# Eighteen whole weight chunks beside the adaLN units instead of six in pieces, and six output blocks parted over the contraction

## What is computed

```python
mod = jax.nn.silu(c) @ ada_w[l] + ada_b[l]              # (9, 2048) @ (2048, 12288)
sh1, sc1, g1, sh2, sc2, g2 = jnp.split(mod[:, None, :], 6, axis=-1)
h = rms_norm(x) * (1.0 + sc1) + sh1
proj = h @ w_in                                          # (288, 2048) @ (2048, 18448)
hq, hf, hi, hg, mq, mk, mv, mi, mf, mo, ga, gb = jnp.split(proj, ...)
# lf = log_sigmoid(mf + bias), ig = mi + bias: the gates; then HGRN2 and mLSTM on these,
# x = x + g1 * (merged @ w_out), a ConvFFN with w_up and w_down, and a last rms_norm
```

## Time and profile before

| | us |
|---|---|
| median of three runs | 2286.97 (2285.03 to 2287.28) |
| span of the profiled execution | 2286.7 |
| PE busy, whole span | 2227.3 (97%) |
| DVE busy, ACT busy, POOL busy | 1091.9, 992.9, 319.4 |
| transpose of the gate rows, the mark at the end of the first stage | starts at 247.41 |

### The profile page before, as it was taken

The page is one execution under the profiler, slowest core; times in us unless marked ns, Lnnn a source line. Parts: engine busy times, 40 slices in busy tenths (PEclk is TensorE's granted clock), DMA queues, the critical chain, the costliest instruction groups (busy, mean ns, idle before and its releaser), DMA issues. The chain is left out here.

```text
span 2286.7 us, 42270 instructions
## 1 busy us (share of the span) xinstructions
PE 2227.3 (97%) x17436; PEld 2084.4 (91%) x17436; DVE 1091.9 (48%) x1454; ACT 992.9 (43%) x1365; POOL 319.4 (14%) x455
## 2 busy tenths in 40 slices
PE   6899999999999999999999997999999999999998
PEld 2489999999999999999999986999999999999997
DVE  1245455464464544444444555555555555544443
ACT  3245553563554334444434445443444343433333
POOL 1010212211221222120211223000000000110000
PEclk8899999999999999999999999999999999999999
DMA  9977676666656576766675779555555555555553
GB/s 344 366 242 220 182 211 186 205 187 206 211 183 198 178 231 194 237 213 205 202 233 180 227 240 317 179 159 172 160 168 160 168 162 166 176 164 172 169 169 107
DMA packets 407411, 460.03 MB, mean 201 GB/s; under 512 B 14844, under 2 KB 379956, under 8 KB 406434
## 3 DMA queue, kind: packets, MB, share of 16 engines
q1 hardware_dynamic: 394192, 410.64, 57.9%
q0 software_dynamic: 12240, 46.03, 6.5%
q10 hardware_dynamic: 833, 1.26, 0.2%
HBM read 431.48 MB, written 26.39 MB: 200 GB/s over the span
## 5 line engine op out<-in xcount | busy, mean ns | idle before, releaser
L697 PE MATMUL ps<-xh,whi 128*128 128x288 f32 x3968 | 1193.4, 301 | 9.8 <-issue 6.2
L1575 DVE TENSOR_TENSOR wlo<-raw,whi 128x1024 fp32r<-128x1024 f32 x584 | 731.3, 1254 | 977.2 <-ACT whi L1161 968.2
L699 PE MATMUL ps<-xh,wlo 128*128 128x288 f32 x3968 | 1172.2, 295 | 0.0
L698 PE MATMUL ps<-xl,whi 128*128 128x288 f32 x3968 | 1171.2, 295 | 0.0
L1161 ACT ACTIVATE whi<-raw 128x1024 fp32r<-128x1024 f32 x584 | 616.5, 1057 | 803.2 <-PE ps L699 773.1
L697 PEld LDWEIGHTS ps<-xh,whi 128*128 128x128 f32 x3968 | 746.7, 188 | 63.2 <-issue 58.9
L698 PEld LDWEIGHTS ps<-xl,whi 128*128 128x128 f32 x3968 | 746.8, 188 | 0.0
L699 PEld LDWEIGHTS ps<-xh,wlo 128*128 128x128 f32 x3968 | 746.5, 188 | 0.0
L697 PE MATMUL ps<-ffh,whi 128*128 128x288 f32 x704 | 209.2, 297 | 0.0
L699 PE MATMUL ps<-ffh,wlo 128*128 128x288 f32 x704 | 208.4, 296 | 0.0
L698 PE MATMUL ps<-ffl,whi 128*128 128x288 f32 x704 | 208.3, 296 | 0.0
(11 more groups left out here) (393 smaller groups left out, 1583.6 us busy)
## 6 DMA issues: line engine op xcount, KB each, us to landing
raw<-in_w_in SPq DMA_DIRECT2D x288, 512.0 KB, 4.3
raw<-in_w_up SPq DMA_DIRECT2D x176, 512.0 KB, 3.6
raw<-in_w_down SPq DMA_DIRECT2D x88, 512.0 KB, 3.5
araw<-in_ada_w SPq DMA_DIRECT2D x74, 512.0 KB, 5.4
raw<-in_w_out SPq DMA_DIRECT2D x32, 512.0 KB, 3.5
uraw_x<-in_ada_w SPq DMA_DIRECT2D x30, 512.0 KB, 8.7
uraw<-in_ada_w SPq DMA_DIRECT2D x24, 512.0 KB, 10.2
top<-in_ada_w SPq DMA_DIRECT2D x24, 512.0 KB, 8.0
```

Source lines behind the costliest of these rows:

```text
L697: mm(o, whi[:, s, kk, cols], hi[:, kt0 + kk, :], start=first and kk == 0, stop=False)
L698: mm(o, whi[:, s, kk, cols], lo[:, kt0 + kk, :], start=False, stop=False)
L699: x = mm(o, wlo[:, s, kk, cols], hi[:, kt0 + kk, :], start=False, stop=last and kk == KC - 1)
L1575: TT(wlo[:, s], raw[:, s], whi[:, s].bitcast(F32), ALU.subtract).then_inc(lo_done, 1)
```

## The change

It works on the first stage alone.

- **Beside the units** stand 18 chunks (`EARLY`) instead of six: PE runs them whole, none or one behind a quarter, from unit 2 on (`BESIDE` = 2). 16 run behind quarters (2, 3, 3, 3, 3, 2 in units 2 to 7), two behind the last unit turn.
- **Six blocks part by part.** Chunks 0 to 23 (`PARTED`) are part 0 of blocks 0 to 5, then part 1 of all six, and so on, so that the first chunks need group 0 alone. Each chunk is its own PSUM group in bank k % 2. Part 0 is copied to `SQ` by ACT, parts 1 to 3 are added to it by DVE (`early_add`, two instructions), and each must be done before chunk k + 2 may write the bank. Chunks 24 to 39 are blocks 6 to 9 as before.
- **Loads.** SP loads chunks 0 to 3 before unit 2, 4 to 7 before unit 3, and 8 to 19 one at a time between the loads of units 4 to 7 (and the end of unit 3), each behind its wait for the low part of chunk k - 4.
- **x.** PE transposes three blocks behind each quarter of unit 0 and four ahead of it; DVE copies them; ACT squares the rows of x with a sum along the row, DVE puts the sums on a diagonal, PE sums with 3 matmuls of 128, 128 and 32 columns in place of 4 of 288. The turn of unit 1 follows that unit directly.
- **POOL** stores `xT` (2.25 MB) after unit 1 and not after unit 7's third quarter, since `SQ` lies over it; the loads of the gates' weights stay where they were.
- **Later** in the stage: gate matmuls from chunk 19, rows of the gates at chunks 23 to 26, `hg_front` at chunks 22 to 30.

```diff
-EARLY = 6
-HG_FIRST = "s" * EARLY + "sssssaa" * 6 + "ssss"
+EARLY = 18
+PARTED = 24
+HG_FIRST = "s" * EARLY + "sssaa" * 6 + "ssss"
...
-    return (n % 2, n // 2) if first and n < 8 else (n // length, n % length)
+    return (n % 6, n // 6) if first and n < PARTED else (n // length, n % length)
...
-BESIDE = 3
-X_AHEAD = 2
-EARLY_PIECES = (0, 1, 1, 2, 1, 1, 1, 1, 0, 1, 1, 2, 1, 1, 1, 1, 0, 2, 2, 2)
+BESIDE = 2
+X_AHEAD = 4
+EARLY_PIECES = (0, 4, 0, 4, 4, 4, 0, 4, 4, 0, 4, 4, 4, 0, 4, 4, 4, 0, 4, 4, 4, 0, 4, 0)
+EARLY_LOADS = 20
+def pieces_ahead(u, h):
+    return sum(EARLY_PIECES[:4 * (u - BESIDE) + h])
+def chunk_ends(u, h):
+    return range(pieces_ahead(u, h) // 4, pieces_ahead(u, h + 1) // 4)
+def loads_ahead(u, c):
+    return RING if u == BESIDE else min(EARLY_LOADS, 2 * RING + pieces_ahead(u - 1, c // 2) // 4)
...
-GATES = 10
+GATES = 19
+ROWS = 23
+FRONT = 5
...
# PE, early chunks
-                    yield from pieces(k + 1, k, part == 0, False, b, xh, xl, KC * part)
+                    pe.wait_ge(bank_free[k % 2], k // 2 + FREE)
+                    yield from pieces(k + 1, k, True, True, k % 2, xh, xl, KC * part)
...
# ACT, beside the units
+            def early_chunk(n):
+                if n < 6:
+                    act.wait_ge(used, n + 1 + FREE)
+                    to_padded(early_tile(n), n % 2)
+                if n + RING < EARLY + LEAD:
+                    hi(N_HG, n + RING)
+            for u in range(BESIDE, UNITS):
+                for h in range(4):
+                    if h == 0 and u in (4, 6):
+                        modulate(1, merged, 0, KT, (u // 2 - 1,))
+                    if h == 3:
+                        unit(u)
+                    for n in chunk_ends(u, h):
+                        early_chunk(n)
...
# DVE
+            def early_add(n):
+                dst, src = early_tile(n), early_bank(n)
+                dve.wait_ge(used, n + 1 + FREE)
+                TT(dst[:, :, 0:TP], dst[:, :, 0:TP], src[:, :, 0:TP], ALU.add)
+                TT(v, v, src[:, :, TP:T].rearrange(...), ALU.add).then_inc(bank_free[n % 2], 1)
...
+            unit(UNITS - 1)
+            k = pieces_ahead(UNITS, 0) // 4
+            early_add(k)
             samples(1, merged, 3, 0, KT)
             low_parts(1, merged, 3)
...
# POOL
-            pool.wait_ge(u_used, 4 * UNITS - 1)
+            pool.wait_ge(u_used, 4 * BESIDE)
             (store of xT, clearing of SQ's padding)
+            pool.wait_ge(u_used, 4 * UNITS - 1)
             (loads of gw, gb, m0)
```

More of the change, by code:

```diff
@@ L120 @@
 N_HG = (0, 0)
+FIRST_PAIRS = PARTED // 2 + 2
 def hg_base(i):
-    return ahead(N_HG, i, 40, 5)
+    return ahead((40, FIRST_PAIRS), i - 1, 40, 5) if i else N_HG
 N_ML = hg_base(4)
@@ L544, in build, with early_bank, early_tile @@
         bias_row = par[:, 0, :]
+        junk = merged[:].rearrange("p a b -> p (a b)")
+        diag = junk[:, 2 * D:2 * D + T]
+        def early_bank(n):
+            return ps[:, n % 2]
+        def early_tile(n):
+            b = place(n, 4, True)[0]
+            return SQ[:, b // 2, 2 * (b % 2):2 * (b % 2) + 2, :]
         rowpad = merged[0:MH, 1:3, :].rearrange("p a b -> p (a b)")[:, 0:TPAD]
@@ L560, in stage @@
                     if kind == "s":
-                        if first and n < EARLY:
+                        if first and n < EARLY_LOADS:
                             continue
@@ L607, in early_load @@
                 load(k, win_v, KC * part, hg_cols(0)[b])
-            for u in range(1, UNITS):
+            for c in range(UC):
+                unit_load(1, c)
+            loaded = 0
+            for u in range(BESIDE, UNITS):
                 for c in range(UC):
+                    for k in range(loaded, loads_ahead(u, c)):
+                        early_load(k)
+                    loaded = loads_ahead(u, c)
                     unit_load(u, c)
-                    if u % 2 == 0 and c % 4 == 3:
-                        early_load(u - 2 + c // 4)
+            for k in range(loaded, EARLY_LOADS):
+                early_load(k)
             hg_stage(0, first=True)
@@ L821, in unit @@
                     x.then_inc(u_used, 1)
-                    if h == 0 and u:
+                    if h == 0 and u not in (0, BESIDE):
                         unit_turn(u - 1)
                     tiles(h)
+                if u == BESIDE - 1:
+                    unit_turn(u)
             def unit_turn(u):
@@ L853, in tiles @@
                         x.then_inc(small_t, 1)
-                    if u == 2 and h == 0:
+                    if u == 1 and h == 0:
                         pe.wait_ge(sq_sum, 3)
-                        for kt in range(4):
-                            x = mm(ab[:, 0:T], ones[:, :], merged[:, kt, :], start=kt == 0, stop=kt == 3)
+                        for t in range(3):
+                            w = P if t < 2 else TS
+                            x = mm(ab[:, P * t:P * t + w], ones[0:w, :], diag[0:w, P * t:P * t + w], start=True, stop=True)
                         x.then_inc(ms_done, 1)
@@ L1043, in _ @@
             pe.wait_ge(ada_free, UNITS + FREE)
-            stream(hg_base(0), HG_FIRST, A_HG, late(GATES, gates(0, "", 0, 0)), xparts=0, start=True)
+            stream(hg_base(0), HG_FIRST, A_HG, late(GATES, gates(0, "", 0, 0)), start=True)
             pe.wait_ge(row_d, ROW_T)
@@ L1237, in conv_state @@
                 A(cst[:, :, 8 * g:8 * g + 8].rearrange("p f r -> p r f"), ab[:, 0:8 * FT].rearrange("p (r f) -> p r f", f=FT), ACT.Copy).then_inc(small_c, 1)
+            act.wait_ge(ld_x, 48)
+            for t in range(3):
+                w = P if t < 2 else TS
+                if t == 2:
+                    act.wait_ge(sq_done, 1)
+                A(junk[0:w, D * (t % 2):D * (t % 2 + 1)], xtm[0:w, t, :], ACT.Square, accum_out=ssx[0:w, t:t + 1]).then_inc(sq_done, 1)
             unit(0)
-            unit(1)
             act.wait_ge(const, 7)
@@ L1305, in stream @@
                     b, part = place(n, 4, start)
-                    if part == 3 and evict is not None:
+                    if start and n < PARTED:
+                        pass
+                    elif start and n == PARTED + 6:
+                        act.wait_ge(used, N[0] + n - 2 + FREE)
+                        evict(6, 0)
+                    elif part == 3 and evict is not None and not (start and b == 6):
                         act.wait_ge(used, N[0] + n + 1 + FREE)
@@ L1310, in stream, with hg_evict @@
                         each(n)
[L1312 to L1317 removed]
+            def hg_evict(g):
                 def evict(u, b):
[L1319 to L1322 removed]
+                    if u == 0:
                         act.wait_ge(hg["cp"], 2 * g)
[L1324 removed]
+                    if u == 4:
                         act.wait_ge(hg["vc"], g)
@@ L1439, in hook @@
                 hg_front(q, 0, True)
[L1440 removed]
+            stream(N_HG, HG_FIRST, A_HG, hg_evict(0), hook, start=True)
             act.wait_ge(row_t, 1)
@@ L1851, in hook, with each @@
                 gate_rows(q)
-                hg_front(q, 0)
-            stream(N_HG, HG_FIRST, A_HG, hook, start=True)
+                hg_front(q - FRONT, 0)
+            def each(n):
+                if n < PARTED:
+                    early_add(n)
+            stream(N_HG, HG_FIRST, A_HG, hook, each, start=True)
             dve.wait_ge(hg["zero"], 3)
```

178 lines of the change are left out of this document (84 added, 94 removed).

## The result

| | before | after |
|---|---|---|
| median of the runs (four each) | 2287.02 us | 2307.71 us (2304.15 to 2308.34) |
| ratio to the kernel before, 95% interval | | 1.0086, 1.0071 to 1.0100 |
| span of the profiled execution | 2286.7 us | 2306.0 us |
| mark: transposes of the gate rows | 247.41 us | 265.19 us |

What follows compares the result with a forecast made beforehand. PE was taken to bound the kernel, and narrowly the end of the units over DMA. A gain of 12.4 us there less 2.8 of waits behind gave 9.6 us: 2277 us from 2286.97, range 2270 to 2286.

Steps and rivals of the forecast that it cites:

- SP's queue: Beside the units, twelve single weight loads each hold a unit's loads 2.1 us, with 5 us of room: cost 0.
- after the units: Behind the units, PE may wait in three places, together 2.8 us, bounds 0 and 8.
- the 85.0: PE's time from the 18th chunk's end to the mark at 247.4, so the change breaks even at 162.4 us.
- term (c): At chunks 23 to 29, ACT's rows, tables and logarithms delay whi, so PE waits 0.9 us for wlo at chunk 29.
- End of the units at 150.0: The 18th chunk ends at 150.0 us, bounded by PE, against 162.4: 12.4 us gained, bounds 17.5 and 6.
- An early chunk is worth 3.2 us: Each chunk moved beside the units saves PE 3.2 us behind them, from 102 matmuls of 0.134 us each.
- evictions by DVE are hidden: 18 DVE sums of 0.9 us each, 16 us in all, hide under PE's 3.2 us a chunk: cost 0.
- rival 4: Beside the units, low parts over 5 us late make unit loads late; twelve waits of 2.1 us: 25 us, 2302, chance 0.07.
- Rival 3: PE waits for DMA at unit starts, falls to 1.2 GHz, loses 3.4 us in each of units 4 to 7: 2291, chance 0.07.
- (a): At the first gate matmul after chunk 19's first piece, PE waits 1.7 us for DVE's gwl.
- (b): Chunk 18's second half needs the second xl at 7.8 and is due at 7.9: 0.2 us.
- rival 2: ACT's pile at chunks 23 to 28 costs 8 us instead of 2.8: 2282, chance 0.14.

Runs made afterwards that it cites:

- e1: Changed kernel with SP's list alone reordered behind the units, ada_w pairs 2 to 6 four weight loads later: 2289.37 us, ratio 0.9997 to the kernel before.
- e13: Changed kernel with SP's list alone reordered, ada_w pairs three weight loads later instead of e1's four: 2289.26 us, ratio 0.9998 to the kernel before.
- e12: e9 plus 40 dummy matmuls ahead of unit 3, with SP's pairs three weight loads later, not four: 2278.98 us, ratio 0.9955 to the kernel before.
- e6: e1 plus 40 dummy matmuls ahead of unit 3's first quarter, results unused: 2287.12 us, ratio 0.9991 to the kernel before.
- e9: e1 with gate rows two chunks earlier and DVE's mod sum and gwl moved forward in its list: 2284.24 us, ratio 0.9979 to the kernel before.

## Why the prediction was wrong

**The step that failed** is the part "SP's queue", and with it the term "after the units". SP's list was looked at where the diff moves it, beside the units, and priced at 0 with a rival for it. Behind the units the only lines of the diff that change SP's list are `EARLY` = 18 and `"sssaa"` for `"sssssaa"`. The prediction took that as a shorter list of chunks, and counted the pairs on PE alone (1.07 us each, inside the 85.0). That each pair is also a load that waits for PE, with the next weights behind it, and that two chunks fewer between two pairs take 6.4 us from the room for that, was in no term and in no rival. The trace of the kernel before has the wait already (SP, 122 to 248 us):

```profile
SPq L577 <- PE ab L722: 31.7, 5, 7.4
```

That wait was free, and how near it was to not being so was not asked. Instead of 2.8 us, PE lost about 26 between the 18th chunk (154.0) and the mark (265.19), which are 111.2 us apart and not 85.0: 19.1 us of waits in the list and some 7 us of low clock behind them. e1 and e13 give 15 and 19 us of them back at the mark by SP's order alone (16.7 and 17.5, counted from the last unit turn). The rest is mostly term (c) below.

**The terms one by one.**

- *85.0 us of PE's work after 18 chunks, break-even at 162.4*: right. In e12 the last unit turn is at 144.90, two chunks and the turn later it is 152.4, and the mark comes at 239.19: 86.8 us, of which 1.0 are waits.
- *End of the units at 150.0*: 4.0 us early. The 18th chunk ends at 154.0 (last unit turn at 146.52, 0.9 for the turn and two chunks). Unit 3's first quarter came at 68.75 (forecast 67.2). From there to unit 4's first quarter 19.25 us passed, with the low clock that had been charged once; in e6, where the clock stayed at 1.00, it was 14.85, near the 14.7 of the forecast, so the low start cost 4.4 here (3.0 in e1), and 3.4 was forecast. The other units took 15.1 to 15.9 us. PE bounded them, as forecast, and from unit 4 on it waited for no load.
- *An early chunk is worth 3.2 us; evictions by DVE are hidden*: right; no wait for a bank over 0.3 us up to 180 us.
- *SP's single waits beside the units, rival 4*: cost 0. The sign that was named for it is there, SP's waits for `wlo` with a fall to 218 GB/s from 80 to 86 us, but PE waited for no load behind it. Rival 4's trigger was sought at the right engine and in the wrong stretch: the time it gave (2302) was near the truth for a reason that it did not have.
- *Rival 3, the clock low at every unit*: did not occur in the changed kernel beyond unit 3's start (e1 had it once more, at 94.91). The Trainium skill (TensorE: Matmul & The Clock Gate, HAM oscillation) describes that case for a kernel whose bursts are shorter than its DMA waits; with three chunks in a unit there were no such waits, and the stretches from 80 us on are at full clock. It did occur behind the units, where idle times of 4.6, 5.5 and 5.3 us lie in stretches with a mean clock of 0.91, 0.83 and 0.83.
- *(a) gwl 1.7 us*: 0.79. *(b) 0.2*: nothing. *(c) the pile of ACT, 0.9*: too small. With SP's order mended it costs 4.36 us of waiting for `mod` and some 3.4 us of low clock behind it (e13: 0.88 and 0.95 in 180 to 220 us), 7.8 us, which is the size of rival 2. The mark of e9, without that wait, is 7.0 us earlier than e13's; by the medians the two edits to the rows and to DVE's list give 4 us (e1 and e9). The error in it: only `whi` and `wlo` were followed through the pile. DVE's `mod` sum stands at its end too, and PE's next pair waits for it. The Trainium skill (PSUM — Partial Sum Buffer, Engine vs sequencer instructions) says that the queues of ScalarE, VectorE and GpSimd are strictly first in, first out; the rows of e13 agree, with an instruction of 0.15 us that ran 7.4 us after PE had its input ready.

**What was right** is the idea of the change, and in part its size. With SP's and DVE's lists mended and no dummy matmuls (e9) the kernel is 4.8 us faster than the kernel before, about half of the 9.6 us of the sum. With the dummy matmuls, which the kernel before did not get, and pairs three loads later (e12) it is 10 us faster, 2279 against 2289, 8.2 of them at the mark. The dummy matmuls have 1 to 2 us of that. What the rest of the step from e9 to e12 comes from is not shown: their intervals overlap, and their profiled executions are within 0.2 us at the mark.
